# First layer: gate table and experts in one program, context rows of u and v gathered together

## The reference, cut to what matters

```python
def peer_ffn(h, w_q, keys, u, v):
    ...
        eidx = jnp.take_along_axis(cidx, sel, axis=-1)
        g = jax.nn.softmax(best, axis=-1)
        act = jax.nn.gelu(jnp.einsum('td,thkd->thk', xb, u[eidx]).astype(jnp.float32))
        return jnp.einsum('thk,thkd->td', (g * act).astype(v.dtype), v[eidx]).astype(h.dtype)
```

## Time and profile before

| | us |
|---|---|
| median of 3 runs | 3096.03 |
| lowest, highest | 3093.18, 3098.45 |
| the profiled execution's own time | 3100.98 |
| its span (first to last instruction) | 3099.2 |

### The profile page before, as it was taken

One profiled execution on the slowest core, in us unless ns is written; L12 is line 12 of the kernel. 1 busy time (PEld: TensorE's weight loads), 2 busy tenths in 40 slices (PEclk: granted clock), 3 DMA queues, 4 the chain that ended last, 5 costly groups with the idle time before them and its releaser, 6 DMA issues. The chain is left out here.

```text
span 3099.2 us, 40897 instructions
## 1 busy us (share of the span) xinstructions
PE 2513.2 (81%) x15178; PEld 1880.7 (61%) x15178; DVE 1965.0 (63%) x4483; ACT 1124.4 (36%) x2244; POOL 1134.1 (37%) x1013
## 2 busy tenths in 40 slices
PE   5978798797558778778799999798797797778776
PEld 3778664575557777667677777587665552223222
DVE  3666663389958899778734433566643798845454
ACT  3431354325753333333333333343343443333332
POOL 1014101331027675556565555202203353434331
PEclk8985698899789999889899999897697899999998
DMA  6210105156169999999999999531003899999996
GB/s 211 79 31 1 63 4 202 61 187 216 82 261 406 407 405 358 394 386 400 368 406 405 406 405 406 200 92 32 9 1 110 363 408 421 422 421 421 421 422 251
DMA packets 211894, 816.89 MB, mean 264 GB/s; under 512 B 22680, under 2 KB 41688, under 8 KB 178032
## 3 DMA queue, kind: packets, MB, share of 16 engines
q0 software_dynamic: 110592, 536.92, 42.9%
q1 hardware_dynamic: 101104, 277.35, 24.3%
HBM read 796.37 MB, written 17.83 MB: 263 GB/s over the span
## 5 line engine op out<-in xcount | busy, mean ns | idle before, releaser
L2046 PE MATMUL ps<-pair_ring,pair_diag 128*128 128x512 f32 x1024 | 475.5, 609 | 142.8 <-ACT pair_diag L2120 142.8
L2230 DVE CUSTOM_DVE_ANT_0 pair_ring<-pair_ring,hT 128x1024 f32<-128x1024 f32 x256 | 313.1, 1223 | 207.8 <-DMA pair_ring<-in_uv_rows,eid 207.8
L2046 PEld LDWEIGHTS ps<-pair_ring,pair_diag 128*128 128x128 f32 x1024 | 186.7, 191 | 420.2 <-ACT pair_diag L2120 230.0
L2010 POOL DMA_INDIRECT pair_ring<-in_uv_rows,eid x256 | 268.3, 1048 | 390.2 <-PE ps L2046 361.6
L2377 POOL DMA_INDIRECT sparse_ring<-in_v_rows,eidT x256 | 285.7, 1116 | 300.5 <-PE ps L2426 228.5
L2377 POOL DMA_INDIRECT sparse_ring<-in_u_rows,eid x256 | 348.8, 1363 | 113.4 <-issue 68.1
L119 PE MATMUL ps<-h_both 128*128 128x256 f32 x1024 | 311.1, 304 | 86.2 <-DVE h_both L2489 74.2
L2515 DVE CUSTOM_DVE_ANT_0 sparse_ring<-sparse_ring,hT 128x1024 f32<-128x1024 f32 x256 | 304.4, 1223 | 49.0 <-DMA sparse_ring<-in_u_rows,eid 43.3
L120 PE MATMUL ps<-h_both 128*128 128x256 f32 x1024 | 300.4, 293 | 0.3 <-issue 0.3
L121 PE MATMUL ps<-h_both 128*128 128x256 f32 x1024 | 299.9, 293 | 0.8 <-issue 0.8
L119 PEld LDWEIGHTS ps<-h_both 128*128 128x128 f32 x1024 | 207.1, 202 | 149.6 <-DVE h_both L2489 91.2
(11 more groups left out here) (416 smaller groups left out, 5216.8 us busy)
## 6 DMA issues: line engine op xcount, KB each, us to landing
peer_u<-in_uT SPq DMA_DIRECT2D x128, 512.0 KB
peer_v<-in_v_rows SPq DMA_DIRECT2D x128, 512.0 KB
ada_slab<-in_ada_w SPq DMA_DIRECT2D x20, 2048.0 KB, 8.3
proj_slab<-in_w_fm SPq DMA_DIRECT2D x38, 512.0 KB
route_slab<-in_w_pq SPq DMA_DIRECT2D x32, 512.0 KB, 5.8
peer_gates<-dense_stage SPq DMA_DIRECT2D x4, 4096.0 KB, 13.0
peer_gates<-peer_gates SPq DMA_DIRECT2D x32, 512.0 KB
out_slab<-in_w_out SPq DMA_DIRECT2D x16, 512.0 KB, 3.7
```

The costliest lines, as they stand in the source:

```text
L2010: nc.gpsimd.indirect_dma_start(out=ring[:, s % R], out_offset=None, in_=d["uv_rows"], in_offset=bass.IndirectOffsetOnAxis(ap=eid[:, s:s + ...
L2046: mm = nc.tensor.matmul(ps[:, 4 + 2 * t + half, :], diag[:, s % DG, :], ring[:, s % R, D_MODEL + half * BANK:D_MODEL + (half + 1) * BANK], ...
L2230: nc.vector.tensor_tensor_reduce(out=row, in0=row, in1=hT[:, s // NS], scale=1.0, scalar=0.0, op0=ALU.mult, op1=ALU.add, accum_out=dots[:, ...
```

## The change

`phase_dense` and `phase_mixed` become one program, `phase_experts`. Its steps:

- SP: the stores of the table, then at once four blocks of `uT` and `v` (`SW = 4`), then the wait for the stores and the gates. A place of `us` is free when `hidden` has used it. `v` of a block is read out of `uv_first`, a new input with rows of `u` and `v` side by side, so its rows of 4 KB lie 8 KB apart.
- POOL: 256 gathers of 1 MB (a row of `u` and one of `v` per partition) into 7 places. The first three are issued when the program starts; the fourth waits for the second store out of the first half of `dense_stage`. From the eighth on, gather `s` waits until row `s-7` has been summed.
- `hidden` is 8 plain f32 matmuls from the loaded block as it is, with tokens `hw` that DVE puts together once (high plus low part). The high and low parts of `u` are gone.
- The context sum is made on DVE, one row at a time: `add_row`, a `scalar_tensor_tensor` of 128x1024 per row (for the first row of a tile a `tensor_scalar`). Gelu and gate of a row are two small ACT instructions of 128x1 (`weight`). `wdiag`, `quad`, the transposed weights and `eidT` are gone.
- Per step two rows are used, three steps behind (`LAG = 3`); 131 steps.
- The semaphores are cleared ahead of `phase_out` instead of between table and experts.

```diff
@@ phase_experts, in place of phase_dense and phase_mixed
+            R = 7
+            LAG = 3
+            SW = 4
+            FREE = 3
+            BACK = NS // 2 + LAG + 4
+            steps = NKEY + LAG
...
                     def _(sp):
-                        for e in range(NKEY):
+                        def load_u(e):
                             if e >= SW:
-                                sp.wait_ge(ulo, e - SW + 1)
+                                sp.wait_ge(act_mm, e - SW + 1)
                             sp.dma_start(us[:, e % SW], d["uT"][e]).then_inc(u_in[e % SW], 16)
...
-                            sp.dma_start(vs[:, e % SW], d["v_rows"][e * P:(e + 1) * P]).then_inc(v_in[e % SW], 16)
+                            sp.dma_start(vs[:, e % SW], d["uv_first"][e * P:(e + 1) * P, D_MODEL:]).then_inc(v_in[e % SW], 16)
...
+                        sp.wait_ge(g_mm, GROUPS)
+                        for e in range(SW):
+                            load_u(e)
+                            load_v(e)
+                        for r in range(2):
+                            sp.wait_ge(stored[r], 16 * (n // (U * UB)))
+                        load_gates(0)
...
                     def _(pool):
+                        for s in range(S):
+                            if s == FREE:
+                                pool.wait_ge(stored[0], 16 * (n // (U * UB)))
                             if s >= R:
-                                pool.wait_ge(*consumed(s - R))
...
+                                pool.wait_ge(sum_done, s - R + 1)
+                            nc.gpsimd.indirect_dma_start(out=ring[:, s % R], out_offset=None, in_=d["uv_first"],
...
                         def hidden(e):
 
-                            pe.wait_ge(ulo, e + 1)
+                            pe.wait_ge(u_in[e % SW], 16 * (e // SW + 1))
...
-                                mm = product(nc, ps[:, e % 2, 0:n], (uh[:, e % 2, k, :], ul[:, e % 2, k, :]),
-                                             (hp[0][:, k, :], hp[1][:, k, :]), k == 0, k == DC - 1)
+                                mm = nc.tensor.matmul(ps[:, e % 2, 0:n], us[:, e % SW, k, :], hw[:, k, :], start=(k == 0), stop=(k == DC - 1))
...
                     def _(act):
+                        def weight(s):
+
+                            act.wait_ge(dot_done, s + 1)
+                            nc.scalar.activation(dots[:, s:s + 1], dots[:, s:s + 1], ACT.Gelu_apprx_tanh).then_inc(sgelu_done, 1)
+                            act.wait_ge(sgelu_done, s + 1)
+                            nc.scalar.activation(dots[:, s:s + 1], dots[:, s:s + 1], ACT.Copy,
+                                                 scale=gate[:, s // NS, s % NS:s % NS + 1]).then_inc(swt_done, 1)
...
                     def _(dve):
+                        def add_row(s):
+                            t, row = s // NS, ring[:, s % R, D_MODEL:]
+                            dve.wait_ge(swt_done, s + 1)
+                            if s % NS == 0:
...
+                            else:
+                                dve.wait_ge(sum_done, s)
+                                nc.vector.scalar_tensor_tensor(out=acc[t], in0=row, scalar=dots[:, s:s + 1], in1=acc[t],
+                                                               op0=ALU.mult, op1=ALU.add).then_inc(sum_done, 1)
...
-                            if step + 1 < NKEY:
-                                u_low(step + 1)
+                            if p >= 0:
+                                dot(2 * p)
                             if 0 <= e < NKEY:
                                 dve.wait_ge(whi, e + 1)
                                 nc.vector.tensor_tensor(wl[:, e % 2], wt[:, e % 2], f32(wh[:, e % 2]), ALU.subtract).then_inc(wlo, 1)
+                            if p >= 0:
+                                dot(2 * p + 1)
+                            if 0 <= e < NKEY:
                                 dve.wait_ge(vhi, e + 1)
                                 nc.vector.tensor_tensor(vl[:, e % 2], vs[:, e % SW], f32(vh[:, e % 2]), ALU.subtract).then_inc(vlo, 1)
...
+                            if p >= 0:
+                                add_row(2 * p)
+                                add_row(2 * p + 1)
```

More of the change, by code:

```diff
@@ new lines, in phase_experts @@
+            (dot_done, sgelu_done, swt_done, sum_done, tr_mm, back_done) = (
+                sem(f"mixed_{x}{l}") for x in ("dot", "sgelu", "swt", "sum", "tr_mm", "back"))
+            with ExitStack() as st:
+                hot_i = sb(st, f"hot_i{l}", [P, 2, U, NKEY])
+                hot_j = sb(st, f"hot_j{l}", [P, 2, U, NKEY])
+                njT = sb(st, f"dense_nj{l}", [P, n + U])
+                sb(st, f"dense_gap{l}", [P, 10192])
+                stage = sb(st, f"dense_stage{l}", [P, 2, NKEY, TB])
@@ L2459, in _ @@
+                        act.wait_ge(neg_done, 2)
+                        columns(0, 0)
+                        table(0, True)
+                        with act.Fori(1, n // (U * UB)) as it:
+                            table(it, False)
+                        for step in range(steps):
+                            e, p = step - 1, step - LAG
                             if 0 <= e < NKEY:
@@ L2477, in _ @@
[L2477 to L2483 removed]
+                            if p >= 0:
+                                weight(2 * p + 1)
@@ L2571, in build @@
                 else:
-                    eid, eidT = (sb(st, f"{x}{l}", [P, nt, PH * TOPK], U32) for x in ("eid", "eidT"))
+                    eid = sb(st, f"eid{l}", [P, nt, PH * TOPK], U32)
                     gate = sb(st, f"gate{l}", [P, nt, PH * TOPK])
```

410 lines of the change are left out of this document (143 added, 267 removed).

## The result

The changed kernel takes 3058.69 us, the median of four runs (3058.07 to 3060.96), beside 3095.3 for the kernel before in the same session. The ratio is 0.9882, with an interval of 0.9865 to 0.9899. That is 36.6 us faster; 61 were forecast. The range of 3008 to 3080 holds it.

The account below looks back on a forecast made before the run. Transfers were taken to bound phase_mixed. An earlier last byte (-56 us) and a shorter end (-5.5) made -61.5; from 3096.0 this gave 3034.5, told as 3035 us, range 3008 to 3080.

Parts of the forecast that it names:

- Rate: DMA in the experts' stage: 411 GB/s, halfway between 406 and 415.5, with gathers in 8 KB rows.
- the two plateaus: Rates in the profile before: 406 GB/s in phase_mixed, 421 in the second layer's gathers of 8 KB a partition.
- DVE per step: DVE's dots, vl, weight parts and two sums: 6.6 us a step, 7.1 if nothing overlaps, against 8.0 of DMA.
- PE: PE per step: hidden 3.7 us as 16 f32 passes, outputs 2.9, quad gone; 6.6 us at full clock.
- ACT: ACT per step: loses the 1.06 us copy of u, gets twice 0.20 + 0.29 us; no change.
- the sum's waits: DVE's sums waiting for ACT's fresh weights: both waits hidden; otherwise up to 2 x 0.5 us, a 7.6 us step.
- C: Rival, PE in the step: plain f32 hidden and lower clock make it slower; at f = 0.4, +54 us, 3150; chance 0.09.
- Ring of 7: Gather places: a turn takes 28 us, leaving 20 us for a transfer of 2.5; DMA engines don't run dry.
- Start: Seven gathers beside the table, first wt at 911, gather 8 at about 924.5 with 14.1 MB loaded, 405.3 left.
- rival B: Gathers beside the table come late, seven rows only behind it: 12 us lost, 3047; chance 0.10.
- End: Last byte at 1910.5, 56 us sooner; then 10 us to the next phase instead of 15.5, 5.5 less.
- The rest: Moved semaphore clearing, two transposes and an eidT copy gone: under 1 us in all, taken as 0.

Follow-up runs that it names:

- e3: Changed kernel with each gather split in two, from separate tables of u and v, 4 KB a partition; 3076.24 us, ratio 0.9926 to the kernel before.
- e4: Changed kernel loading only the first four blocks of uT and v, all steps working on these; 2924.46 us, ratio 0.9436 to the kernel before.
- e6: Changed kernel with 5 ring places in place of 7; 3056.88 us, ratio 0.9865 to the kernel before.
- e13: Changed kernel with 4 ring places, not 7, and two blocks, not four, ahead of the first gates; 3093.36 us, ratio 0.9976 to the kernel before.
- e9: Changed kernel with LAG = 1, not 3, and two blocks, not four, ahead of the first gates; 3059.7 us, ratio 0.9865 to the kernel before.
- e14: Changed kernel with 5 ring places, three blocks in flight (SW = 3) and two blocks ahead of the first gates; 3058.04 us, ratio 0.9864 to the kernel before.
- e2: Changed kernel with two blocks, not four, issued ahead of the first gates; 3057.75 us, ratio 0.9867 to the kernel before.
- e7: Changed kernel with v's blocks read from a table of their own, without the 8 KB stride; 3062.2 us, ratio 0.988 to the kernel before.

## Why the prediction came out as it did

The mechanism held: transfers bind the stage, no engine takes their place, the 8 KB rows and even steps lift the rate. Two terms of the sum were mis-sized.

- *Rate*, forecast 411, measured 412. Right. e3 splits it: even steps bring 395 to 406, gathers of larger rows 406 to 412. By the Trainium skill (DMA: Bandwidth & Descriptors, "Why small descriptors are slow") a fixed cost of 3 cycles a packet would give the gathers 1.1%, an estimate of 0.7% for the mixture. The runs show 1.5% on the mixture (e3, with twice the gathers), more than this cost alone; the 3.7% between the two plateaus, on 64% of the bytes, would be 2.3%, which is too high.
- *DVE per step*, 6.6, measured 6.84 (e4: 6.83). A sum takes 1.28 us, not 1.23, and two small gaps stand in a step. It costs nothing while bytes take 7.96. *PE*, *ACT* and *the sum's waits* held: 16 passes of `hidden` in about 3.6 us, clock 0.91; C did not come.
- *Ring of 7*: it suffices, by two places (e6, e13). The word that DVE would wait mostly for a row was wrong: it waits for blocks. The 20 us of slack were right, but gathers and blocks don't share alike, 12 us against 25.
- *Start*, the first mis-sized term. Forecast: 30.9 MB moved by 924.5 (14.1 loaded, 16.8 of table stored), a loss of 53 us from the table's begin and a full rate behind it; measured 61.1. Up to 924.5 the trace loses just what was forecast (238 GB/s over the 126.0 us from 798.49, a loss of 53.2); the other 8 us come behind that. The step that failed is the wait of `wt(0)`: I let it wait for block 0 alone. It waited for the gates, behind a store that took 16 us instead of 13, and stood at 923.97 instead of 911. So the first sums, and with them gather 8, came at 935.23 instead of 924.5, and until then little was asked of the DMA engines (920 to 940 us, a loss of 7.7; in e9, with gather 8 at 923.89, 1.8). I also let seven gathers run beside the table, while `FREE = 3` holds four back until `stored[0]`, at 885. This resembles rival B, by a wait in the program, but by 924.5 their bytes had been made up; whether they delayed the store no run shows. For B's other reason, the shared port of the Trainium skill (SBUF — State Buffer, "Who interferes with whom"), the trace shows no sign beside the `tensor_scalar` that I had named: the second and third gather were issued in 0.94 and 0.95 us at 802 and 803 us, with DVE at work on `hot_i`, no longer than the one at 891 with DVE at rest (0.93). It does show one beside another kind of DVE operation, told in the last section; POOL has time for it. What the start gains can be lost again at the end: in e9 the 8.0 us were.
- *End*, the second. Forecast: 411 GB/s to the last byte and 10 us from there to the next phase; measured a loss of 21.6, of which 3 before the last byte, at 1923.5, and 18.5 behind it. The step that failed is the thought that at the last byte only one row's work is left. Blocks are asked for up to four steps ahead, rows seven places ahead, and DVE takes 6.84 us a step whatever lies ready. So when the last bytes are in, DVE still has six sums, four dots and the sums into `xT` to do, and these are sixteen in 5.29 us, not eight in 3.2. Before that only gathers are asked for, two of 1.05 MB in 6.84 us, 307 GB/s at most. With five places (e6) the last byte lands at 1934.2, so 11.5 us lie behind it and 9.5 before it, the same sum. Neither three rows less (e13) nor one block less (e14) is shown to make start and end together lose less than in e2.
- *The rest*, forecast 0: the table begins 2.2 us later and what follows the stage is 1.9 us shorter.

Added up: start 8.1, end 11.6, rate and bytes together -0.6, table and rest 0.3, so 19.4 us, and -61.5 + 19.4 = -42.1; the two profiles differ by 42.0. The forecast of 3035 also took off 5 us because the profile of before stood above its median; the profile of after doesn't, and 19.4 and these 5 are the 24 us by which it was short. What stays open is why the stalls of blocks fall differently at the end in runs that differ only in their start (21.6, 29.4, 26.5 for after, e9, e7); each was profiled once, and medians of after, e2, e6, e9 and e14 differ by less than their intervals. For the same reason no version here is shown to beat the changed kernel.

## What to carry to other kernels

For a stage bound by transfers, keep a ledger against its best rate: lost at the start, in the plateau, at the end; an event that comes 11 us sooner is worth only the bytes that then flow sooner. At the end count how fast the slowest engine still asks for transfers, and what it has left to do on all that has landed, not the work of one last row. A gain at one end is real only if the other end keeps it. And an instruction that is moved ahead keeps the waits written in front of it: read each one before its time is counted as hidden.

## What the runs showed of the hardware

- With both queues full a gather of 1 MB in rows of 8 KB landed after 12.1 us, a plain load of 0.5 MB after 22.7 to 25.2. With rows of 4 KB, in two gathers, it turned about: gathers 15.4 and 18.9 us, loads 8.0 and 10.5. The DMA issues of e3, 1000 to 1900 us:

```profile
peer_v<-in_uv_first SPq DMA_DIRECT2D x111, 512.0 KB, 8.0
peer_u<-in_uT SPq DMA_DIRECT2D x111, 512.0 KB, 10.5
...
pair_ring<-in_v_rows,eid POOLq DMA_INDIRECT x222, 18.9
pair_ring<-in_u_rows,eid POOLq DMA_INDIRECT x221, 15.4
```

So the form of the gathers decides how the two queues share the engines, and which buffer is short. Whether it is the size of a row or the number of gathers isn't shown, as e3 changes both.

- A `tensor_scalar` of 128x1024 f32 took 0.75 us, a `scalar_tensor_tensor` of the same size 1.28.
- POOL takes longer to issue a gather when DVE is at work on an operation with two inputs in SBUF. Timeline of POOL and DVE in the changed kernel:

```profile
799.22 2.46 POOL L2262 DMA_INDIRECT pair_ring<-in_uv_first,eid  x1 [67.20 <-POOLq L1618]
799.24 1.43 DVE L2389 TENSOR_TENSOR hot_j<-jT,iota 128x1280 f32<-128x1280 f32 x1
...
801.99 0.94 POOL L2262 DMA_INDIRECT pair_ring<-in_uv_first,eid  x1 [0.30 <-issue]
...
887.94 2.30 DVE L2427 TENSOR_TENSOR peer_h<-h_both 128x2048 f32<-128x2048 f32 x1
887.95 3.10 POOL L2262 DMA_INDIRECT pair_ring<-in_uv_first,eid  x1 [0.31 <-issue]
```

The extra time, 1.5 and 2.2 us over 0.94, is about what was left of the DVE operation (1.4 and 2.3). From 939 to 1900 us the 18 gathers issued with DVE at rest took 0.93 to 0.94 us, and 123 of the 124 issued beside a sum 1.93, with 1.1 us of the sum left; those issued in the last 0.3 us of a dot took 1.17. A `tensor_scalar` at work (801.99) added nothing. It looks as if the gather waits for that one operation to end; this is read from the trace, and no run tests it. POOL is busy for 342 of 900 us here, so it costs nothing.
